# Up products of a gated feed-forward from seven half products instead of eight (Strassen), in a two-layer hybrid backbone

## The reference, cut to what matters

```python
def conv_ffn(h, w_up, conv_w, conv_b, w_down):
    u = dwconv_centered(h @ w_up, conv_w, conv_b)
    g, v = jnp.split(u, 2, axis=-1)
    return (jax.nn.silu(g) * v) @ w_down
...
        xs = xs + mod_s[5][..., None, :] * conv_ffn(modulate(xs, norm_ffn_g[l], mod_s[3], mod_s[4]), *ffn)
```

## Time and profile before

| | |
|---|---|
| median of 3 runs (range) | 1881.08 us (1880.3 to 1882.69) |
| profiled execution: span | 1880.0 us |
| profiled execution's own time | not given apart from its span |
| TensorE / VectorE / ScalarE / GpSimd busy | 97% / 53% / 32% / 63% |
| first feed-forward | 309.2 to 803.4 us |
| second feed-forward | 1389.8 to 1865.4 us |
| DMA | 208.66 MB, mean 111 GB/s |

### The profile page before, as it was taken

One profiled execution on the slowest core, in us unless ns is written; L12 is line 12 of the kernel. 1 busy time (PEld: TensorE's weight loads), 2 busy tenths in 40 slices (PEclk: granted clock), 3 DMA queues, 4 the chain that ended last, 5 costly groups with the idle time before them and its releaser, 6 DMA issues. The chain is left out here.

```text
span 1880.0 us, 33251 instructions
## 1 busy us (share of the span) xinstructions
PE 1815.3 (97%) x12789; PEld 1713.1 (91%) x12789; DVE 994.1 (53%) x1589; ACT 602.4 (32%) x1149; POOL 1189.6 (63%) x869
## 2 busy tenths in 40 slices
PE   6999999999999999989999999989999999999997
PEld 5878799999999999979889898868999999999997
DVE  4556754662256236364666666587346623651552
ACT  4245421220022012143765856574112201220221
POOL 2533466777777777746555455534877778777774
PEclk9999999999999999989999999989999999999999
DMA  9631164424243424434333433243222222222212
GB/s 357 210 123 39 33 227 151 162 76 159 68 156 88 147 88 136 157 101 116 112 102 113 128 93 117 79 123 101 78 70 69 77 72 74 78 67 78 75 54 84
DMA packets 256188, 208.66 MB, mean 111 GB/s; under 512 B 7352, under 2 KB 235741, under 8 KB 255453
## 3 DMA queue, kind: packets, MB, share of 16 engines
q1 hardware_dynamic: 255373, 204.69, 34.6%
q10 hardware_dynamic: 720, 2.62, 0.4%
HBM read 196.63 MB, written 10.67 MB: 110 GB/s over the span
## 5 line engine op out<-in xcount | busy, mean ns | idle before, releaser
L1027 POOL TENSOR_SCALAR w_hi<-raw 128x512 fp32r<-128x512 f32 (+1 forms) x430 | 640.8, 1507 | 669.1 <-PE ps L1069 510.5
L1031 POOL TENSOR_TENSOR w_lo<-raw,w_hi 128x512 fp32r<-128x512 f32 (+1 forms) x430 | 548.6, 1297 | 0.0
L1069 PE MATMUL ps<-h_hi,w_hi 128*128 128x324 f32 (+1 forms) x1432 | 345.2, 322 | 2.9 <-DVE h_lo L2451 2.9
L1069 PE MATMUL ps<-h_hi,w_lo 128*128 128x324 f32 (+1 forms) x1432 | 329.0, 311 | 0.0
L1069 PE MATMUL ps<-h_lo,w_hi 128*128 128x324 f32 (+1 forms) x1432 | 327.6, 310 | 0.0
L1069 PEld LDWEIGHTS ps<-h_hi,w_hi 128*128 128x128 f32 x1432 | 241.4, 190 | 20.6 <-issue 20.3
L1069 PEld LDWEIGHTS ps<-h_hi,w_lo 128*128 128x128 f32 x1432 | 240.6, 189 | 0.0
L1069 PEld LDWEIGHTS ps<-h_lo,w_hi 128*128 128x128 f32 x1432 | 240.3, 189 | 0.0
L2341 DVE SCALAR_TENSOR_TENSOR xT<-ps,mod,xT 128x128 f32 (+1 forms) x112 | 56.6, 547 | 270.9 <-PE ps L1069 265.5
L1069 PE MATMUL ps<-g_hi,w_hi 128*128 128x324 f32 (+1 forms) x816 | 188.6, 312 | 5.0 <-POOL w_lo L1031 3.3
L1069 PE MATMUL ps<-g_hi,w_lo 128*128 128x324 f32 (+1 forms) x816 | 187.2, 310 | 0.0
(11 more groups left out here) (372 smaller groups left out, 3087.2 us busy)
## 6 DMA issues: line engine op xcount, KB each, us to landing
raw<-in_ffn_w_up SPq DMA_DIRECT2D x88, 512.0 KB, 3.9
ada<-in_ada_w SPq DMA_DIRECT2D x40, 1024.0 KB, 6.4
raw<-in_ssd_w_in SPq DMA_DIRECT2D x40, 512.0 KB, 4.1
raw<-in_ffn_w_down SPq DMA_DIRECT2D x32, 512.0 KB, 3.9
R<-scr_acs SPq DMA_DIRECT2D x22, 512.0 KB, 4.9
raw<-in_att_w_in SPq DMA_DIRECT2D x16, 512.0 KB, 6.7
ada_att<-in_ada_w SPq DMA_DIRECT2D x8, 1024.0 KB, 7.0
raw<-in_ssd_w_out SPq DMA_DIRECT2D x16, 512.0 KB, 4.1
```

Of the source, the lines that this page charges most:

```text
L1027: nc.gpsimd.tensor_scalar(w_hi[slot][:, a_:b_, :], raw[j][:, a_:b_, :], 1.0, None, ALU.mult).then_inc(w_hi_done, 1)
L1031: ins = nc.gpsimd.tensor_tensor(w_lo[slot][:, a_:b_, :], raw[j][:, a_:b_, :], w_hi[slot][:, a_:b_, :].bitcast(F32), ALU.subtract)
L1069: ins = mm(out[:, cols], w[slot][:, k, :], x[:, cols], start=first and k == 0 and i == 0, stop=last and k == n - 1 and i == 2)
```

## The change

Gate tile and value tile of unit i together are a 2 x 2 block product: weights W11, W21 (gate, k slices 0 to 3 and 4 to 7), W12, W22 (value), activations cut into k slices 0 to 3 and 4 to 7 and into columns left (322) and right (322). Strassen's form (Winograd's variant) needs seven products, each of 4 k slices x 3 = 12 matmuls of 322 columns:

- P1 to P4 take a raw weight block or s4, P5, P6, P7 take weight sums st (twice) and s3. Their right operands are b11, b21, b22 (blocks of h) and t1 to t4 (differences of blocks), each kept as a high part and a remainder (c_hi, c_lo).
- P6, P7 and P4 are accumulated on P1 in the same bank; ScalarE copies P1 and P5 out before that (copy_p1, copy_p5), and VectorE joins (up_left, up_sum, up_right, low_right).
- VectorE forms the weight sums (chain_1 to chain_4) and the remainders of st; ScalarE makes all high parts (job_high); GpSimd makes only remainders: of five of seven weight jobs (job_lo), of the hidden tile (hidden_low), and of b21, b22, t3, t4.
- The activations are now normalised, shifted and split before the first product (prepare). scale, side_pads and the bias trick go.
- Weights come in half tiles (256 KB a DMA) and half slots: job j+4 is split when job j is done. Down jobs are halves of a tile (24 matmuls).
- In layer 0 modulation rows 6 to 10 are made in twenty small steps inside the units (ada_side, side_add); row 5 is made in the preparation. GpSimd begins the scan's weights only when the last job is done. Some semaphores and buffers are shared or moved.

The core of the diff, TensorE's order and waits first:

```diff
+    for p, (m0, n) in enumerate(PARTS):
+        jobs += [("P", 1, m0), ("P", 2, m0), ("P", 5, m0)]
+        for i in range(m0, m0 + n - 1):
+            jobs += [("P", 6, i), ("P", 1, i + 1), ("P", 2, i + 1), ("P", 7, i), ("P", 3, i), ("P", 5, i + 1),
+                     ("P", 4, i)]
+        i = m0 + n - 1
+        jobs += [("P", 6, i), ("P", 3, i), ("P", 7, i), ("D", p, 0, 0), ("P", 4, i), ("D", p, 1, 0), ("D", p, 2, 0),
+                 ("D", p, 0, 1), ("D", p, 1, 1), ("D", p, 2, 1)]
+        jobs += [("D", p, m, half) for m in range(3, KD) for half in range(2)]
...
+            def product(l, x, i):
...
+                if x in (1, 5):
+                    if i >= m0 + 2:
+                        pe.wait_ge(value_free, g - 1)
+                    elif p:
+                        pe.wait_ge(dn_free, 24 * l + 8 * (p - 1) + (7 if i % 2 else 6))
+                elif x == 2:
+                    if i >= m0 + 2:
+                        pe.wait_ge(gate_free, g - 1)
...
+                elif x == 6:
+                    pe.wait_ge(c11_done, g + 1)
+                elif x == 7:
+                    pe.wait_ge(u4_done, g + 1)
+                else:
+                    pe.wait_ge(c22_done, g + 1)
...
+                for k in range(4):
+                    if i == 0:
+                        comb_wait(l, x, k)
+                    for n_, (w, c) in enumerate(((wh, ch), (wh, cl), (wl, ch))):
+                        ins = mm(out, w[:, k, :], c[:, k, :], start=x in (1, 2, 3, 5) and (k, n_) == (0, 0),
+                                 stop=x in (2, 3, 4, 5) and (k, n_) == (3, 2), skip_group_check=True)
+                        if l == 0 and i in ADA_SIDE and x in (1, 2) and (k, n_) == (0, 0):
+                            ada_side(i, x - 1)
```

ScalarE's preparation and its order in the units:

```diff
+                for k in range(4):
+                    add_shift(k)
+                    act.wait_ge(h32_done, 8 * l + k + 1)
+                    high_of("b11", slice(k, k + 1), h32[:, k:k + 1, 0:HW])
+                for k in range(4, 8):
+                    add_shift(k)
+                    act.wait_ge(h32_done, 8 * l + k + 1)
+                    high_of("b21", slice(k - 4, k - 3), h32[:, k:k + 1, 0:HW])
+                high_t("t1", 1)
+                high_of("b22", slice(0, 4), h32[:, 4:8, HW:WS])
+                high_t("t2", 2)
+                copy_p1(l, 0)
+                high_t("t3", 3)
+                high_t("t4", 4)
...
+                    if x == 4:
+                        value_id(l, i)
+                        if i + 2 < m0 + n:
+                            copy_t(l, i + 2)
+                        silu(l, i)
+                    high_job(j + 4)
+                    if x == 1 and i > m0 + 1:
+                        hidden_high(l, i - 2)
...
+                    if x == 1 and i:
+                        copy_p1(l, i)
+                    if x == 5:
+                        copy_p5(l, i)
+                    if x == 3:
+                        gate_id(l, i)
```

VectorE's preparation (the second half of it) and its order in the units:

```diff
+                for k in range(KD):
+                    normalise(l, k)
+                    if 1 <= k < 5:
+                        b11_low(l, k - 1)
...
+                combine(l, "t1", h32[:, lo4, right], h32[:, lo4, left])
+                chain_2_low(l, 0)
+                comb_low(l, "t1", lo4, t32["t1"][:, :, :], 9)
...
+                combine(l, "t2", h32[:, hi4, right], t32["t1"][:, :, :])
+                up_left(l, 0)
+                comb_low(l, "t2", lo4, t32["t2"][:, :, :], 11)
+                combine(l, "t3", h32[:, hi4, right], h32[:, lo4, right])
...
+                combine(l, "t4", h32[:, hi4, left], t32["t2"][:, :, :])
...
+            def period(l, i):
...
+                if i > m0:
+                    value_taps(l, i - 1)
+                if i + 1 < m0 + n:
+                    chain_1(l, i + 1)
+                if i > m0:
+                    hidden(l, i - 1)
+                if i + 1 < m0 + n:
+                    up_sum(l, i)
+                    chain_1_low(l, i + 1)
+                    chain_2(l, i + 1)
+                    up_left(l, i + 1)
+                    chain_3(l, i + 1)
+                    chain_4(l, i + 1)
+                    low_right(l, i)
+                    chain_2_low(l, i + 1)
+                    up_right(l, i)
...
+                gate_taps(l, i)
```

GpSimd:

```diff
+                for j in range(2):
+                    low_of(j)
+                for k in range(4):
+                    comb_low(n, "b21", slice(k, k + 1), h32[:, 4 + k:5 + k, 0:HW], 5 + k)
+                comb_low(n, "b22", slice(0, 4), h32[:, 4:8, HW:WS], 10)
+                comb_low(n, "t3", slice(0, 4), t32["t3"][:, :, :], 12)
+                comb_low(n, "t4", slice(0, 4), t32["t4"][:, :, :], 13)
+                for j, job in enumerate(JOBS):
+                    low_of(j + 4)
+                    if job[0] == "P":
...
+                        if job[1] == 2 and i > m0 + 1:
+                            hidden_low(l, i - 2)
...
+            ffn(0)
+            pool.wait_ge(job_mm, N_JOBS)
+            splits(T_E, T_O, 1)
```

More of the change, by code:

```diff
@@ new lines, with part_of, block_of, ffn_loads @@
+JOBS = ffn_schedule()
+JOB_AT = {job: j for j, job in enumerate(JOBS)}
+N_JOBS = len(JOBS)
+LO_POOL = [job for job in JOBS if job[0] == "D" or job[1] not in (5, 6)]
+LO_POOL_AT = {job: j for j, job in enumerate(LO_POOL)}
+def part_of(i):
+    return next(p for p, (m0, n) in enumerate(PARTS) if m0 <= i < m0 + n)
+def block_of(job):
+    if job[0] == "D":
+        return job[2] % 4, job[3]
+    i = job[2]
+    return {1: (2 * (i % 2), 0), 2: (2 * (i % 2), 1), 4: (2 * (i % 2) + 1, 1)}[job[1]]
+def ffn_loads():
+    out = []
+    for p, (m0, n) in enumerate(PARTS):
+        out += [("P", what, i) for i in range(m0, m0 + n) for what in (1, 2, "21", 4)]
+        out += [("D", p, m, half) for m in range(KD) for half in range(2)]
+    return out
@@ L680, in build @@
         acc_ends, count = [], {"act": 0, "dve": 0}
-        for a_ in range(A_F1 + FFN_TILES):
+        for a_ in range(A_O + 8):
             who = "dve"
@@ L921, in row_loads @@
+            ffn(0)
+            for b in range(4):
+                sp.wait_ge(lo_pool, lo_pool_done(0, ("D", 2, 4 + b, 1)))
             def row_loads(n, d_):
@@ new lines, in up_left, with up_sum @@
+            def up_left(l, i):
+                dve.wait_ge(p1_copied, FT * l + i + 1)
+                dve.wait_ge(job_mm, job_done(l, ("P", 2, i)))
+                if l == 0 and i in ADA_SIDE:
+                    side_add(i)
+                tt(py(i), py(i), p1c, ALU.add).then_inc(c11_done, 1)
+            def up_sum(l, i):
+                dve.wait_ge(p5_copied, FT * l + i + 1)
+                dve.wait_ge(job_mm, job_done(l, ("P", 6, i)))
+                tt(su4[:, :], px(i), p5c, ALU.add).then_inc(u4_done, 1)
@@ new lines, in downs @@
+            def downs(l, p):
+                m0, n = PARTS[p]
+                first = m0 + n
+                value_taps(l, m0 + n - 1)
+                hidden(l, m0 + n - 1)
+                dve.wait_ge(mod_done, 6 + 6 * l)
+                for m in range(KD):
+                    dve.wait_ge(job_mm, job_done(l, ("D", p, m, 1)))
+                    residual(l, 5, m, DN_SLOT[m], dn_free)
+                    if l == 0 and m == 4:
+                        for row in ADA_TURNS[p]:
+                            mod_evac(row, 2, 2 * P * (row % 2))
+                        if p == 1:
+                            gain(2, 8)
+                        if p == 2:
+                            gain(3, 11)
+                    if p < 2 and m == 5:
+                        chain_1(l, first)
+                    if p < 2 and m == 6:
+                        chain_1_low(l, first)
+                        chain_2(l, first)
+                        chain_3(l, first)
+                        chain_4(l, first)
+                    if p < 2 and m == 7:
+                        chain_2_low(l, first)
+                        up_left(l, first)
+                    if (l, p) == (0, 2):
+                        if m >= 2:
+                            add_square(2, m - 1, sq[(m - 1) % 2])
```

1000 lines of the change are left out of this document (607 added, 393 removed).

## The result

The changed kernel takes 1934.01 us (median of 4 runs, 1933.61 to 1935.14) against 1880.69 (1878.9 to 1882.69, 4 runs): ratio 1.0283, 95% interval 1.0268 to 1.0297. It is slower by 2.8%; 1930 us, 2.6%, was forecast. The profiled execution took 1933.65 us, its span is 1931.8; the span before was 1880.0, so 51.8 us are to be found.

A forecast was written before the change was run, and what follows sets the result against it. TensorE, busy 97% of the span, was taken to bound the kernel. Terms -77.9 + 46.4 + 9 + 71.3 + 3.7 - 3 = +49.5 us gave span 1929.5, time 1930 us, slower by 2.6%; range 1893 to 1957.

The forecast's parts named there:

- removed matmuls: Feed-forward products: 44 units x 12 matmuls fewer at 147.6 ns each, -77.9 us if nothing waits.
- value tile's wait: Inner units: P1 of the next unit waits for VectorE's value taps, 1.45 us, 32 times, +46.4 us.
- P7's wait: Last unit of each part: P7 waits for up_sum, 6 x 1.5 us, +9 us (bounds 5 and 12).
- the two heads: Start of each layer's products: TensorE held by the preparation, +33.5 and +37.8 us, together +71.3.
- side steps: Layer 0 units: twenty modulation steps at 1.1 us replace five bursts, +3.7 us (0 to +18).
- part switches: Layer 1's idle 4.3 us mostly goes, as half jobs cross the last unit: -3 us.
- rival 4: Inner units: the value tile's wait does not bite, 1930 - 46 = 1884 us, same; chance 0.05.
- VectorE, ScalarE and GpSimd inside the unit: Per unit 11.2 (0.6 more in layer 0), 9.1 and 7.9 us of work, all fitting in 13.9: costed at nothing.
- Rival 3: VectorE becomes the bound of a unit: 14.6 us, x 44 = +31, time 1961 us; chance 0.14.
- The preparation: Each layer's head: activations prepared with TensorE empty, ScalarE taking 1.63 us a slice; layer 0's P1(1) at 44.8 us; +71.3.
- Rivals 1 and 2: Layer heads: 1, short preparation, +16.7 in place of +71.3, chance 0.08; 2, held only until P2 ends, 1898, chance 0.15.
- t2 and b22: Layer heads: VectorE's t2 is blocked by GpSimd's b22 for its remaining 2.9 us; fair port sharing would give 1928.

The follow-up runs named there:

- experiment 1: Changed kernel with product P3 put between P6 and the next unit's P1 in the inner units: 1890.42 us.
- experiment 5: Changed kernel with VectorE's up_sum ahead of the hidden product in the last unit of each part: 1924.98 us.
- experiments 4 and 6: Changed kernel with s4 made twice in each inner unit: 1934.07 us; changed kernel with the hidden tile's remainder back on VectorE: 1933.68 us.
- experiment 10: Kernel of experiment 8 with the hidden remainder back on VectorE and s4 made twice in each inner unit: 1888.49 us.
- experiment 11: Changed kernel with ScalarE's shift of the 512-column part left out in both preparations: 1929.22 us.
- experiment 2: Changed kernel with the head's weight halves (jobs 4 to 6) ahead of combinations t2, t3, t4 on ScalarE and GpSimd: 1920.78 us.
- experiment 3: Changed kernel with one added wait, so GpSimd starts b22's remainder only when VectorE has made t2: 1928.79 us.
- experiment 7: Changed kernel with half the columns of each side step's matmuls left out (64 of 128): 1923.42 us.
- experiment 8: Changed kernel with experiment 1, experiment 2, experiment 3 and experiment 5 together, b22 after t3, job 7 ahead of t4: 1864.08 us.

## Why the prediction was right

The balance of the two spans, term by term. The part switches are what the other terms leave of the two stages, so the sum closes by them and does not test them:

| step | forecast | measured | from |
|---|---|---|---|
| removed matmuls | -77.9 | -77.9 | count |
| 3696 products' matmuls, 322 columns | 0 | +4 | 148.8 ns, not 147.6 |
| value tile's wait, 32 | +46.4 | +43.6 | experiment 1 |
| P7's wait, 6 | +9 | +8 | 6 x (1.09 + 0.24), experiment 5 |
| the two heads | +33.5, +37.8 | +30.9, +36.0 | timelines |
| side steps | +3.7 | +10 to +12 | 20 x 1.53 against five bursts of 3.66 to 3.96 |
| part switches | -3 | -5 to -7 | the rest |
| outside the feed-forwards | 0 | +2 | windows |
| sum | +49.5 | +52 | span: +51.8 |

- **Removed.** Right in count, slightly off in price: the 147.6 ns was read from matmuls of 324 and 318 columns in turn, 321 on the mean, and the new ones have 322. That column makes 0.5 of the 1.2 ns; where the rest comes from is open.
- **The value tile's wait.** Right, in place, count and mechanism; 1.45 us a wait was forecast, 1.36 measured. The 13.9 us unit came out at 13.85. The small miss is the restart: it was put at 0.2 us from a pair of 0.56, but that pair follows the modulation burst without a gap, and the 0.88 of rows 9 is a pair at half clock. Drain (0.16) and restart together measure 0.24. Experiment 1 excludes that the gap had another cause, and rival 4 with it.
- **P7's wait.** 1.5 forecast, 1.3 measured: the hidden product took 1.37 us where I took the median of before, 1.613.
- **VectorE, ScalarE and GpSimd inside the unit.** Costing them at nothing was right (experiments 4 and 6); VectorE was busy 10.2 us, 74% of the unit, in layer 1, and 10.9 of 15.4 in layer 0, not 11.2 and not "about 85%". Rival 3 was wrong for this kernel, and right as a limit: with 11.9 us of work for a 12.5 us unit VectorE's queue does decide (experiment 10).
- **The preparation.** The chain of steps was right; each step came a little sooner: P5, P6 and P1(1) in layer 0 at 24.6, 32.5 and 42.2 us where 26.1, 34.3 and 44.8 were forecast, because a slice takes 1.46 us on the mean, not 1.63. One claim in it was not right: ScalarE alone does not pace the slices (experiment 11). Net: 42.2 less 7.1 of products, less the 6.2 of before, and 2.0 for the clock: 30.9; layer 1, 43.6 - 7.1 - 2.9 + 2.4 = 36.0. The 2.0 and 2.4 are what the 72 matmuls from P1(1) on took over the same work later on (13.1 us against 10.7 in layer 1), the clock still being at half at their start; the same stretch took 12.2 to 13.6 us in the other kernels that leave it alone, so this term is known to a microsecond. Rivals 1 and 2 were excluded by P1(1) at 42 us, ended by GpSimd as forecast; experiment 2 shows that its last 6 us were the order on GpSimd's and ScalarE's queues.
- **t2 and b22.** Forecast: t2 is blocked for b22's length. It was (4.00 against 1.49 us, experiment 3), and this agrees with the rule cited from the Trainium skill, page "SBUF — State Buffer", section "Who interferes with whom".
- **Modulation.** The failed term. "Most is column-bound: 1.1 x 20" left out what two interruptions of the stream of products cost: 1.53 us a step were measured, some 0.85 of columns and 0.7 of interruptions (experiment 7). It lay within the bounds given (0 to +18). Its DMAs are two of 512 KB a unit (40 in all), not of 256 KB as the prediction has it; no wait of TensorE in the units is put down to them, and the DMA share of the stage stayed at 0.38.

So the mechanism was as forecast. That the time came within 4 us is luck in part. Terms of +7 (side steps), +4 (price of a matmul) and +2 (outside) were missed on one side, and of -3 (value tile's wait), -4 (heads), -1 (P7) and -3 (part switches) on the other, and they nearly cancel: the span is 2.3 us over the forecast one. Another microsecond is the 1.1 added to the span, where the profiled execution took 1.85 more than its span. The eighth product was worth its 78 us; 44 went into the value tile's waits, 67 into the two heads and 8 into six waits at the part ends. That most of this was a property of the order, not of the algorithm, is shown by experiment 8: 70 us came back without a computation removed. What is left of the heads' cost (67 less 18) was probed by experiment 11, not repaired.

## What to carry to other kernels

When fewer matmuls make a stage shorter, list for each accumulator what must happen between its last matmul and the first one that overwrites it, and put that much work of TensorE between the two in the order; here one product more did it. In a preparation that TensorE waits for, write each engine's queue in the order of need of the consumer, and keep two-operand operations of VectorE and GpSimd on SBUF apart in time. A spare engine is spare only for the unit as long as it is now: redo that sum after each repair.

## What the runs showed of the hardware that was not expected

- A wait of 1.12 us on a filled TensorE costs 1.36: 0.24 us for emptying and refilling, on the mean of the 32 waits that experiment 1 takes away. An interruption by 16 small matmuls of a side step costs some 0.34 us beside its columns (estimated from experiment 7).
- VectorE's t2 took 4.00 us beside one GpSimd operation of 2.85, longer than its own 1.49 by 2.5, while the GpSimd operation was hardly longer than alone (2.71); the same 128x642 product took 1.613 in the median before and 1.37 in the units now; the cause of that difference was not tested.
- Side steps of 64 columns save 0.43 us of 1.53 each against 128 columns: more than half of a side step is paid by columns, if these are paid in proportion.
- TensorE's granted clock was 0.50 in the 4.6 us from P1(1) on where 6.15 us of waiting stood before P1(1), and 1.00 in the 4 us from P1(1) on where that gap was gone (layer 1, experiment 2). So a repaired wait can be worth more than its idle time.
